# Order of steps, block places and branch-weight slots in the mixer part of a two-block transformer kernel

## The chip, the cores and the metric

The kernel runs as one program on one core of a Trainium2 chip. The metric is device time in microseconds (us) of one execution, as the median of several. The engines' names are those of the profile: PE (matmul), PEld (its weight loads), DVE (VectorE), ACT (ScalarE), SP (the queue that issues nearly all DMAs).

## The reference, cut to what matters

The input is 256 tokens of 1024 float32. A first block of two layers is followed by a second block (latent attention, mLSTM, 16 experts). Only the first block's layers are touched:

```python
for layer in range(2):
    h = rms_norm(x, norm1_g[layer])
    cols = lambda lo, w: h @ w_in[layer][:, lo:lo + w]
    y_sb   = stick_breaking_attention(...)          # from cols(0, 768)
    y_rwkv = rwkv7_time_mix(cols(768, 1024), ...)   # recurrence over 256 tokens
    y_moba = moba_attention(...)                    # from cols(1792, 768)
    y_hgrn = hgrn2_mixer(...)                       # from cols(2560, 1024)
    merged = 0
    for n, y_n in enumerate((y_sb, y_rwkv, y_moba, y_hgrn)):
        gate = sigmoid(cols(3584 + n * 1024, 1024))
        merged += gate * (y_n @ w_branch[layer, n])     # w_branch: 256 x 1024
    x = x + merged @ w_out[layer]
    h2 = rms_norm(x, norm2_g[layer])
    x = x + (silu(h2 @ w_ffn_gate) * (h2 @ w_ffn_up)) @ w_ffn_down
```

RWKV's recurrence is computed in two chunks of 128 tokens. Each needs the inverse of a unit lower triangular 128x128 matrix per head; it is built by doubling: from D (the diagonal blocks of 2) to blocks of 128 in six levels. HGRN's pair scores are built over eight levels of block size.

## The kernel before

All matrices lie with features on the 128 partitions and tokens along the row. `w_in` is multiplied in three products of a high and a low part (`group3`): ACT copies a weight block to the rounded high part (`block_high`), DVE subtracts to get the low part (`block_low`), PE multiplies. A *block* is 128 columns of `w_in`, all 1024 rows (1024 floats a partition). Two blocks come in one DMA of 1 MB to a *quarter slot*. There are four of these: the halves of ring slots 0 and 1. Slot 2 holds high parts only, in four block places up to block 28 (`TWO_PLACES`); from there on in two places, and its other half (slot `HALF`) takes first the weights of branch 1 and then, one after the other, the rows of `w_mod_2` that the second block will need (`modulation`; 8 loads in layer 0, 16 in layer 1). Low parts replace the weights in the quarter slot.

A layer runs so:

1. RWKV's 8 input blocks (unsplit float32, line 1223), with RWKV's first steps at places given by `EARLY_STEPS`, and on ACT and DVE the splits of the first blocks.
2. `mix([rw], fill, RW_PLAN)`: RWKV's steps, one at a time. After each, as many *fill steps* as the plan says. A fill step is half a unit of the other input columns: 12 matmuls of 256 columns on PE; on ACT and DVE what goes with it (an eviction, the high part of a block ahead, the low part of a block ahead). Steps 0 to 9 are first steps, keys, masks; 24 steps are the doubling; 8 the end of RWKV.
3. `branch(l, 1)`: RWKV's result by its branch weights.
4. `mix([hgrn, stick, moba], fill, MX_PLAN[l])`: the three other mixers in turn, one step of each, with fill steps between, now also modulation steps (`woven`: one after every 4 fill steps in layer 0, after every 2 in layer 1).
5. `branch` 0, 2, 3, then `w_out`, then the feed-forward jobs.

Every engine has its own program, written in the same order of steps by the same `mix` and plans; nothing is reordered at run time. An engine waits where its next instruction needs another's result, and all that is written behind it waits too. `take` gives PSUM banks in turn and waits for the bank's last reader. In `sync_program`, `load` takes the least recently used slot of the allowed ones and waits until what it holds has been used; SP issues strictly in the order written. Before branches 0, 2 and 3 are loaded, `ring_of` returns to the three full slots. So branch 0 goes to slot 0 (`held[0] = held[QUARTERS[1]]`: the last gate weights of that quarter), the next to slots 1 and 2, and `w_out` waits for the branches that use those slots.

In the row names, `ring` is loaded weights, `rring` the split high and low parts, `rgates` and `rarena` the split input, `ps` a PSUM bank, `high` and `low` the working memory.

## Time and profile before

| | us |
|---|---|
| median of 3 runs | 2205.24 (2203.21 to 2205.80) |
| profiled execution | 2205.08 |
| its span | 2203.3 |
| PE busy | 1869.2 (85%) |
| DVE busy | 908.7 (41%) |
| ACT busy | 639.8 (29%) |

Layer 0 runs from 0 to about 651 us of the span, layer 1 to about 1300 us; the second block follows, and its experts are the last third, in which 16 DMA engines are busy most of the time. In the two layers PE is busy in nearly every slice, and no single other engine is. A busy PE counts pipelined matmuls up to their modelled ends, so the idle time ahead of an instruction, with what ended it, tells more than the share.

### The profile page before, as it was taken

Reading aid. Unit: us, or ns where it says so; the run is one execution under the profiler, and the core shown is the slowest. Engines: PE = TensorE matmul, PEld = TensorE weight load, DVE = VectorE, ACT = ScalarE, POOL = GpSimd, SP = SyncE. Lnnn points to the kernel's source line nnn. Section 1 sums busy time; section 2 is a strip of 40 time slices with the busy share of each in tenths; the row PEclk is TensorE's granted clock in tenths of the full one; section 3 lists DMA queues with packets and bytes.
Section 4 is the critical chain, followed back from the end, with each engine's and each line's share of the span. In section 5 each row is a group of like instructions: output and inputs, shape, how many; then the busy total and the mean of one; then the engine's idle time right before and its main releaser. Section 6 shows DMA issues by size and latency. Waiting matters only on the chain.

```text
span 2203.3 us, 28203 instructions
## 1 busy us (share of the span) xinstructions
PE 1869.2 (85%) x12094; PEld 1447.0 (66%) x12094; DVE 908.7 (41%) x1432; ACT 639.8 (29%) x900; POOL 0.2 (0%) x4
## 2 busy tenths in 40 slices
PE   6899888899998899788999999998999875555555
PEld 5799776699996898666799999545788521111101
DVE  3665453556635754443546665413344300000001
ACT  3423242144433322322144454333442210000000
POOL 0000000000000000000000000000000000000000
PEclk9999999999998999997999999999999998887888
DMA  6323340555433323651565451121026899999997
GB/s 214 128 97 112 118 153 20 180 186 188 164 125 103 108 96 115 209 174 70 207 191 165 171 158 63 60 74 39 6 74 235 354 409 409 409 409 409 409 409 302
DMA packets 199645, 414.27 MB, mean 188 GB/s; under 512 B 5472, under 2 KB 119392, under 8 KB 196064
## 3 DMA queue, kind: packets, MB, share of 16 engines
q1 hardware_dynamic: 198800, 408.69, 51.0%
q10 hardware_dynamic: 720, 3.78, 0.4%
q8 instruction: 95, 1.56, 0.3%
q14 instruction: 30, 0.25, 0.0%
HBM read 411.41 MB, written 1.05 MB: 187 GB/s over the span
## 4 chain that ended last, share of the span: by engine, by line
PE 51%; DMA 21%; DVE 16%; ACT 9%; issue 2%; SPq 1%; DVEq 0%; ACTq 0%
PE ps L219 37%; PE ps L825 7%; DVE rarena L178 5%; ACT rarena L213 5%; DMA ring<-in_w_e_down_dram 5%; DMA high<-in_w_e_up_dram 4%; DMA high<-in_w_e_down_dram 3%; DVE low L178 3%; DVE high L178 3%; PE ps L1585 2%; DMA high<-in_w_e_gate_dram 2%; DMA ring<-in_w_e_gate_dram 2%; ACT high L213 2%; DMA ring<-in_w_mod_dram 2%; DVE high L188 1%
## 5 line engine op out<-in xcount | busy, mean ns | idle before, releaser
L219 PE MATMUL ps<-rarena 128*128 128x256 f32 (+1 forms) x3648 | 459.9, 288 | 9.6 <-DVE rarena L178 7.4
L219 PEld LDWEIGHTS ps<-rarena 128*128 128x128 f32 x3648 | 448.2, 192 | 19.6 <-DVE rarena L178 10.4
L219 PE MATMUL ps<-rgates,rring 128*128 128x256 f32 x1472 | 313.7, 301 | 5.3 <-DVE rring L178 5.3
L213 ACT ACTIVATE high<-ps 128x512 f32<-128x512 f32 (+2 forms) x226 | 109.3, 484 | 623.0 <-PE ps L1585 286.7
L219 PEld LDWEIGHTS ps<-rgates,rring 128*128 128x128 f32 x1472 | 250.1, 200 | 21.2 <-issue 14.0
L1585 PE MATMUL ps<-high,low 128*32 128x512 f32 x1040 | 162.4, 755 | 111.6 <-DMA high<-in_w_e_up_dram 38.3
L178 DVE TENSOR_TENSOR rarena<-ring,rarena 128x2048 fp32r<-128x2048 f32 x76 | 167.3, 2201 | 137.5 <-ACT rarena L213 135.9
L219 PE MATMUL ps<-rarena,rring 128*128 128x256 f32 x736 | 214.9, 292 | 0.0
L213 ACT ACTIVATE rarena<-ring 128x2048 fp32r<-128x2048 f32 x76 | 139.9, 1841 | 150.0 <-DMA ring<-in_w_ffn_up_dram 85.7
L1585 PEld LDWEIGHTS ps<-high,low 128*32 128x32 f32 x1040 | 31.4, 126 | 227.8 <-issue 59.7
L825 PE MATMUL ps<-high 128*128 128x128 f32 (+6 forms) x1024 | 131.5, 304 | 36.8 <-DVE high L178 32.2
L178 DVE TENSOR_TENSOR high<-high,ps 128x512 f32<-128x512 f32 x52 | 35.7, 687 | 301.0 <-PE ps L1585 266.6
L219 PEld LDWEIGHTS ps<-rarena,rring 128*128 128x128 f32 x736 | 147.7, 201 | 0.5 <-issue 0.5
L825 PEld LDWEIGHTS ps<-high 128*128 128x128 f32 (+2 forms) x1024 | 110.6, 196 | 50.5 <-DVE high L178 21.1
L219 PE MATMUL ps<-low,ring 128*128 128x256 f32 (+1 forms) x544 | 128.6, 393 | 16.3 <-DMA ring<-in_w_branch_dram 9.8
L178 DVE TENSOR_TENSOR rring<-ring,rring 128x1024 fp32r<-128x1024 f32 x104 | 127.4, 1225 | 32.5 <-ACT rring L213 23.5
L219 PE MATMUL ps<-high,ring 128*128 128x256 f32 (+1 forms) x544 | 132.8, 396 | 0.9 <-ACT low L213 0.9
L213 ACT ACTIVATE rring<-ring 128x1024 fp32r<-128x1024 f32 x104 | 110.1, 1059 | 80.2 <-PE ps L219 74.9
L1585 PE MATMUL ps<-ring,low 128*32 128x512 f32 x496 | 78.8, 768 | 58.8 <-DMA ring<-in_w_e_down_dram 20.1
L219 PEld LDWEIGHTS ps<-low,ring 128*128 128x128 f32 (+1 forms) x544 | 99.7, 190 | 43.8 <-DMA ring<-in_w_branch_dram 10.2
L219 PE MATMUL ps<-high 128*128 128x64 f32 (+7 forms) x576 | 123.5, 353 | 4.7 <-DVE high L192 3.9
L219 PEld LDWEIGHTS ps<-high,ring 128*128 128x128 f32 x544 | 100.8, 190 | 28.1 <-issue 11.4
(159 smaller groups left out, 1705.4 us busy)
## 6 DMA issues: line engine op xcount, KB each, us to landing
ring<-in_w_in_dram SPq DMA_DIRECT2D x66, 1024.0 KB, 5.2
high<-in_w_e_gate_dram SPq DMA_DIRECT2D x22, 2048.0 KB, 23.9
high<-in_w_e_up_dram SPq DMA_DIRECT2D x22, 2048.0 KB, 23.9
high<-in_w_e_down_dram SPq DMA_DIRECT2D x21, 2048.0 KB, 24.1
ring<-in_w_mod_dram SPq DMA_DIRECT2D x24, 1024.0 KB, 4.9
ring<-in_w_ffn_gate_dram SPq DMA_DIRECT2D x22, 1024.0 KB, 5.4
ring<-in_w_ffn_up_dram SPq DMA_DIRECT2D x22, 1024.0 KB, 8.0
ring<-in_w_e_down_dram SPq DMA_DIRECT2D x11, 2048.0 KB, 24.2
```

Of the source, the lines that this page charges most:

```text
L178: return self.e.tensor_tensor(out, x, y, op)
L188: return self.e.scalar_tensor_tensor(out=out, in0=x, scalar=s, in1=y, op0=op0, op1=op1)
L213: return self.e.activation(out, x, f, scale=scale, **kw)
L219: ins = self.e.matmul(out, l, r, start=first and i == 0, stop=end and i == n - 1)
L825: return PE.e.matmul(out, l, r, start=True, stop=True)
L1585: ins = PE.e.matmul(bs[ch][32 * e_:32 * e_ + 32, :], lhs(k, e_), w[:, e_, 512 * ch:512 * ch + 512], start=k == 0, stop=k == 7)
```

## The change

`EARLY_STEPS` and `RW_PLAN` steps of RWKV come ahead of the splits in the input loop on ACT and DVE, and the splits there start one turn (ACT) or two turns (DVE) later. DVE's keys move from two steps before the copies to a place right behind the bonus product. D is made in two halves, each with a name of its own (`D00`, `D01`). `TWO_PLACES` goes from 28 to 32. Branch 1 and then branches 0, 2 and 3 are loaded to quarter slots in turn; the full slots follow for `w_out` and the feed-forward weights. `RW_PLAN` gives 18 fill steps in the doubling where it gave 24; `MX_PLAN` gives fewer in the first rounds of the mixers and three to each step from the 28th on. HGRN has an empty step before its last product on each engine.

```diff
-        assert len(BLOCK) == BLOCKS and first_block["g00"] == TWO_PLACES
+        assert len(BLOCK) == BLOCKS and first_block["g01"] == TWO_PLACES
...
@@ sync_program
-            def branch(l, n, at=None):
+            def branch(l, n):
                 load(f"{l}b{n}", (lambda t: t[:, 0:2048].rearrange("p (k n) -> p k n", k=2),
-                                  a["w_branch"][l, n].rearrange("(k p) n -> p k n", p=128)), at=at)
+                                  a["w_branch"][l, n].rearrange("(k p) n -> p k n", p=128)))
...
                 for n, ch in GATES[0:3]:
                     gate(l, n, ch)
+                branch(l, 1)
                 held[HALF] = f"{l}blk{TWO_PLACES - 1}.used"
-                branch(l, 1, at=HALF)
                 mods = modulation(l)
...
-                ring_of[0] = range(NSLOT)
-                held[0], held[1] = held[QUARTERS[1]], held[QUARTERS[3]]
-                held[2] = f"{l}fill.used"
                 for n in (0, 2, 3):
                     branch(l, n)
+                ring_of[0] = range(NSLOT)
+                held[0], held[1], held[2] = held[QUARTERS[1]], held[QUARTERS[3]], f"{l}fill.used"
+                for i in (2, 1 - l, l):
+                    recent.remove(i)
+                    recent.append(i)
@@ hgrn of tensor_program and of scalar_program; in vector_program behind placed(7)
                     yield
+                yield
@@ scalar_program, input loop
-                    if 4 <= n < 7:
-                        block_high(l, n - 4)
                     if n in EARLY_STEPS[l]:
                         next(rw)
+                    if n > 4:
+                        block_high(l, n - 5)
@@ vector_program, rwkv
                 V.tt(R.bo, v2(ps(f"{l}bo.ps")), R.v, mul).then_inc(*V(f"{l}bo"))
                 yield
-                yield
                 V.wait_ge(f"{l}ee")
...
                 V.tt(R.KB[:, 1, :, :], R.k, R.en, mul).then_inc(*V(f"{l}KB"))
+                yield
                 yield
...
-                V.tt(R.D, R.Lm, bc8(c("lev", 0)), mul).then_inc(*V())
-                V.tt(R.D, R.D, bc8(c("ident")), add).then_inc(*V())
-                V.tt(R.DT, R.M4[:, :, 0:128], bc8(c("levt", 0)), mul).then_inc(*V())
-                V.tt(R.DT, R.DT, bc8(c("ident")), add).then_inc(*V(f"{l}D00", f"{l}D01"))
+                bc4 = lambda z: z.unsqueeze(1).to_broadcast([128, 4, 128])
+                for z in range(2):
+                    h = slice(4 * z, 4 * z + 4)
+                    V.tt(R.D[:, h, :], R.Lm[:, h, :], bc4(c("lev", 0)), mul).then_inc(*V())
+                    V.tt(R.D[:, h, :], R.D[:, h, :], bc4(c("ident")), add).then_inc(*V(f"{l}D0{z}"))
+                for z in range(2):
+                    h = slice(4 * z, 4 * z + 4)
+                    V.tt(R.DT[:, h, :], R.M4[:, h, 0:128], bc4(c("levt", 0)), mul).then_inc(*V())
+                    V.tt(R.DT[:, h, :], R.DT[:, h, :], bc4(c("ident")), add).then_inc(*V(f"{l}DT0{z}"))
@@ vector_program, input loop
-                    if n in (4, 5):
-                        block_low(l, n - 4)
                     if n in EARLY_STEPS[l]:
                         next(rw)
+                    if n > 5:
+                        block_low(l, n - 6)
@@ tables
-BLOCKS, TWO_PLACES = 52, 28
+BLOCKS, TWO_PLACES = 52, 32
-RW_PLAN = [3, 4, 3, 4, 3, 1, 1, 1, 1, 3] + 24 * [1] + [1, 1, 1, 1, 1, 2, 2, 3]
-MX_PLAN = 13 * [2] + [1], 22 * [2] + [1]
+RW_PLAN = [3, 4, 3, 4, 3, 1, 1, 1, 1, 3] + 6 * [1, 1, 0, 1] + [1, 1, 1, 1, 1, 2, 2, 3]
+MX_PLAN = [2] + 26 * [1] + [3], 9 * [2, 1, 1] + [3]
```

DVE's order in layer 0 around the keys (the reciprocal of 128x4 and the seven instructions behind it are the keys; `rring<-ring,rring` is a low part; the first row is the bonus product; the last two are the gated columns and the start of the forget gates):

```order
 L178 TENSOR_TENSOR high<-ps,high 128x512
-L178 TENSOR_TENSOR rring<-ring,rring 128x8x128 x2
+L178 TENSOR_TENSOR rring<-ring,rring 128x8x128
+L196 RECIPROCAL high<-high 128x4
+L188 SCALAR_TENSOR_TENSOR high<-high 128x2x128
+L178 TENSOR_TENSOR high<-high 128x2x128
+L188 SCALAR_TENSOR_TENSOR high<-high 128x2x128
+L178 TENSOR_TENSOR high<-high 128x2x128
+L178 TENSOR_TENSOR high<-high 128x512 x3
+L178 TENSOR_TENSOR rring<-ring,rring 128x8x128
 L188 SCALAR_TENSOR_TENSOR high<-high,ps 128x256 x2
 L200 MEMSET low 128x2
```

Before, the keys stood 15 rows behind the bonus product, after the forget gates' preparation and one more low part; now they are two rows behind it, and one of the two low parts follows them.

DVE's order in the doubling of layer 0, two levels. Before (`high<-ps,low` evicts an X with its mask, `high<-high,ps` adds to D or DT):

```order
L178 TENSOR_TENSOR high<-ps,low 128x512
L178 TENSOR_TENSOR high<-high,ps 128x512 x2
L178 TENSOR_TENSOR rring<-ring,rring 128x8x128
L178 TENSOR_TENSOR high<-high,ps 128x512 x2
L178 TENSOR_TENSOR high<-ps,low 128x512
L178 TENSOR_TENSOR rring<-ring,rring 128x8x128
L178 TENSOR_TENSOR high<-ps,low 128x512
```

The same place after:

```order
L178 TENSOR_TENSOR high<-ps,low 128x512
L178 TENSOR_TENSOR high<-high,ps 128x512 x4
L178 TENSOR_TENSOR rring<-ring,rring 128x8x128
L178 TENSOR_TENSOR high<-ps,low 128x512 x2
L178 TENSOR_TENSOR rring<-ring,rring 128x8x128
L178 TENSOR_TENSOR high<-high,ps 128x512 x4
```

The low part between the additions has gone, and three low parts stand where two levels had four.

DVE's order in layer 0 at HGRN's end (`high<-ps 128x256 x2` takes the last level, `high<-ps 128x512` HGRN's product, `low<-ps 64x256` a head of stick or MoBA, `low<-ps 2x512` the modulation's rows):

```order
-L192 COPY low<-ps 2x512 x4
+L178 TENSOR_TENSOR rring<-ring,rring 128x8x128
 L192 COPY high<-ps 128x256 x2
+L178 TENSOR_TENSOR rring<-ring,rring 128x8x128
+L192 COPY low<-ps 64x256
+L178 TENSOR_TENSOR rring<-ring,rring 128x8x128
+L192 COPY low<-ps 64x256
+L178 TENSOR_TENSOR rring<-ring,rring 128x8x128
 L192 COPY high<-ps 128x512
 L178 TENSOR_TENSOR high<-high 128x512
```

Three low parts and two heads now lie between HGRN's last level and its product, and the copies of the modulation's rows come later. SP's queue has the same DMAs in the same order before and after; only what each waits for differs.

## Rows read from the trace of the kernel before

**Rows 1.** The page: its head and section 1.

```profile
span 2203.3 us, 28203 instructions
PE 1869.2 (85%) x12094; PEld 1447.0 (66%) x12094; DVE 908.7 (41%) x1432; ACT 639.8 (29%) x900; POOL 0.2 (0%) x4
```

**Rows 2.** Timeline of PE: start, duration, engine, instruction, [idle before <- releaser].

```profile
43.60 0.76 PE L825 MATMUL ps<-low,high 65*128 65x256 f32 x1 [8.62 <-DVE high L200]
```

**Rows 3.** Timeline of DVE, layer 0, before that wait's end.

```profile
41.85 1.23 DVE L178 TENSOR_TENSOR rring<-ring,rring 128x1024 fp32r<-128x1024 f32 x1
43.19 0.27 DVE L200 MEMSET high<- 1x256 f32 x1
```

**Rows 4.** Timeline of PE, layer 0: the copies of keys, the first X.

```profile
99.79 0.47 PE L821 MATMUL ps<-cst,high 128*128 128x128 f32 x1 [6.91 <-DVE high L178]
...
126.69 0.38 PE L825 MATMUL ps<-high 128*128 128x128 f32 x1 [2.73 <-DVE high L178]
```

**Rows 5.** Timeline of DVE, layer 0: keys, mask products, D.

```profile
89.09 0.42 DVE L188 SCALAR_TENSOR_TENSOR high<-high,ps 128x256 f32<-128x256 f32 x1 [3.05 <-ACT high L213]
...
97.13 0.43 DVE L178 TENSOR_TENSOR high<-high 128x256 f32<-128x256 f32 x1
...
108.19 0.69 DVE L178 TENSOR_TENSOR high<-ps,cst 128x512 f32<-128x512 f32 x1 [1.57 <-PE ps L825]
...
110.88 0.69 DVE L178 TENSOR_TENSOR high<-ps,cst 128x512 f32<-128x512 f32 x1 [1.20 <-PE ps L825]
...
121.63 1.23 DVE L178 TENSOR_TENSOR high<-high,low 128x1024 f32<-128x1024 f32 x1
```

**Rows 6.** Windows, PE instructions with tile rring (fill steps), in the doubling.

```profile
127.00:192.00 65.00, 40.08 (x288) 1.00 0.27 89
```

**Rows 7.** Timeline of PE, layer 0, last fill steps before branch 1.

```profile
224.63 0.55 PE L219 MATMUL ps<-rgates,rring 128*128 128x256 f32 x1 [2.66 <-DVE rring L178]
```

**Rows 8.** Windows: PE, PEld, DVE, ACT, POOL busy (instructions), granted clock, DMA.

```profile
229.00:310.00 81.00, 72.09 (x533) 60.80 (x534) 39.30 (x66) 30.43 (x46) 0.00 (x0) 0.96 0.45 156
310.00:395.50 85.50, 67.40 (x457) 55.73 (x455) 33.12 (x57) 21.21 (x38) 0.00 (x0) 0.92 0.15 53
867.00:950.00 83.00, 70.19 (x523) 55.64 (x522) 38.88 (x69) 27.10 (x42) 0.00 (x0) 0.98 0.52 178
950.00:1043.00 93.00, 77.97 (x537) 61.26 (x535) 36.95 (x62) 24.52 (x43) 0.00 (x0) 0.89 0.34 116
994.00:1007.50 13.50, 13.50 (x61) 9.99 (x60) 1.89 (x6) 2.41 (x4) 0.00 (x0) 0.55 0.13 39
```

**Rows 9.** Timeline of PE: waits in the mixers.

```profile
297.49 0.38 PE L825 MATMUL ps<-high 64*128 64x128 f32 x2 [0.53 <-DVE high L178]
...
343.46 0.38 PE L825 MATMUL ps<-high 64*128 64x128 f32 x2 [3.56 <-DVE high L178]
...
357.04 0.32 PE L219 MATMUL ps<-high 128*128 128x64 f32 x1 [3.89 <-DVE high L192]
...
379.14 0.33 PE L821 MATMUL ps<-cst,high 128*128 128x128 f32 x1 [1.94 <-DVE high L183]
...
993.12 0.59 PE L825 MATMUL ps<-high 64*128 64x128 f32 x2 [3.52 <-DVE high L178]
...
1025.67 0.33 PE L821 MATMUL ps<-cst,high 128*128 128x128 f32 x1 [2.28 <-DVE high L183]
```

**Rows 10.** Timelines of SP's queue and of PE: loads of branch weights.

```profile
390.57 0.89 SPq L690 DMA_DIRECT2D ring<-in_w_branch_dram  x2
...
395.53 0.80 PE L219 MATMUL ps<-low,ring 128*128 128x256 f32 x1 [5.00 <-DMA ring<-in_w_branch_dram]
...
1043.05 0.79 PE L219 MATMUL ps<-low,ring 128*128 128x256 f32 x1 [4.84 <-DMA ring<-in_w_branch_dram]
```

**Rows 11.** Waits: engine, who waited for whom, us in total, times, longest.

```profile
PE ps L878 <- DMA ring<-in_w_mod_dram: 6.7, 7, 1.8
```

**Rows 12.** Timeline of ACT, behind the exponentials, a high part.

```profile
89.15 1.06 ACT L213 ACTIVATE rring<-ring 128x1024 fp32r<-128x1024 f32 x1
```

More of the change, by code:

```diff
@@ L2235, in rwkv @@
                 V.tt(R.KB[:, 1, :, :], R.k, R.en, mul).then_inc(*V(f"{l}KB"))
+                yield
                 yield
@@ L2378, in hgrn @@
                 placed(7)
+                yield
                 V.wait_ge(f"{l}hy.ps")
```

## The prediction

> **What bounds the kernel now.** I read the page first: PE is busy 85% of the span, DVE 41% [rows 1]. The last third is the expert stage, where weights stream in; nothing in it is edited, so it only starts earlier or later. I then listed every PE wait above 0.25 us in the PE timeline from 0 to 1280 us. The feed-forward jobs wait about 0.5 us apiece and are untouched. What is left is the mixer part of each layer, and I cut it by windows. The doubling (127 to 187 us) has no PE idle at all; between branch 1 and branch 0 PE idles 8.9 and 18.1 us in layer 0, 12.8 and 15.0 us in layer 1, which is each window less its PE busy time [rows 8]. Since PE's work does not change, the whole question is how much PE idle time goes or comes. I take layer 0 for the working and say where layer 1 differs.
>
> **1. First steps ahead of the splits.** PE waits 8.62 us for the one-row memset of RWKV's first step [rows 2]; on DVE a low split of 1.23 us stands right before it [rows 3]. Moved behind it, the memset comes 1.3 us earlier, in both layers. But DVE then has three low splits in a row where two stood, ahead of the operand of PE's next RWKV product, the norm of the keys; block 1's split, which DVE did early while it waited, is the third. 1.3 us won, 1.23 us more in front of the operand: I take 0. Bounds: 0 to -1.3 us a layer.
>
> **2. Keys ahead.** PE waits 6.91 us for the keys in layer 0 [rows 4], less in layer 1. The keys' eight instructions take 4.2 us on DVE; their last four are the 2.61 us that end at 99.74, 0.05 before PE goes on. Their operand, the exponentials of ACT, is there at about 89.1, since ACT is at its next instruction by 89.15 [rows 12] and DVE takes up work at 89.09 [rows 5]. So they end at 93.3 us and PE's wait shrinks to some 0.5 us. That is not the gain. In this stretch DVE is the later engine: from 89.09 on it waits for nothing but 1.21 us for ACT, and the split that came before and now comes behind the keys fills those. The other moved work only changes places, and PE next waits for the two splits behind the keys (an estimate of 0.3 and 2.3 us in layer 0). What PE's lead is worth is DVE's own waits for PE that follow, at the mask products: 1.57 and 1.20 us [rows 5]. They go: -2.8 us. Bounds: nothing, to the full 6.91.
>
> **3. D in halves.** Four instructions of 1.23 us become eight of 0.69 [rows 5]: with the 0.03 us between instructions 5.04 becomes 5.76, +0.7 us on DVE. PE's 2.73 us wait in front of the first X [rows 4] goes, but PE then only waits two steps later for X's own evictions, which stand behind all eight instructions and one split; I count no gain. Parts 2 and 3 together: -2.1 us a layer, -4.2 in all. The Trainium skill, "VectorE: DVE Perf Modes", section on the errata, says that each VectorE instruction reading SBUF pays a fixed latency that a large tile pays once and many small ones each; it speaks against this edit, and the trace agrees: half the elements take 56% of the time, not half. By its rule the edit costs 4 x 0.15 us a layer, the 0.7 of rows less the spacing; nothing in the sum hangs on it.
>
> **4. Doubling with 18 fill steps for 24.** A fill step is 12 matmuls, 40.08 us / 24 = 1.67 us, some 1.5 where it overlaps its neighbours [rows 6]. Six of them leave: the doubling gets 9 us shorter and the mixers 9 us longer, net 0. Is PE still covered? Without the fill step between the two D/DT groups a level has 11.0 - 1.5 = 9.5 us of PE work; DVE has six adds or products of 0.69 and on average one and a half splits of 1.23 in it, about 6.5 us, and each X is evicted while PE works through a fill step. I take no new wait; the bound is 0.5 us a level, +6 for both layers.
>
> **5. Four block places until block 32.** Before, PE waits 2.66 us in layer 0, and as long in layer 1, for a split that DVE has behind RWKV's last evictions [rows 7]: blocks 28 to 31 already run on two places, one ahead. With four places to block 31 and only 58 instead of 64 fill steps before branch 1, that split is long done. -5.3 us. Branch 1's weights, in a quarter slot now, need units 24 and 25 used; six fill steps and RWKV's last products, over 12 us, still lie between that and branch 1, and such a load takes about 5 us from issue to use (390.57 to 395.53 [rows 10]).
>
> **6. Branch weights.** The three loads of branches 0, 2 and 3 are issued together at 390.57, when the last fill unit has been used, and PE waits 5.00 us in layer 0 and 4.84 in layer 1 [rows 10]. In quarter slots the load of branch 0 only needs units 44 and 45 used and comes in SP's queue behind the last modulation load; in both layers four mixer steps or more of three fill steps remain, over 15 us. Both waits go: -9.8 us. The two halves of w_out are issued later than these and PE does not wait for them before either.
>
> **7. Fill moved from the first chains to the last.** Layer 0 gives two steps, then one to each of 26 mixer steps, then three; layer 1 gives two to each HGRN step and one to the others, for 9 rounds, then three. At the end PE waits 3.89 (HGRN's last product), 1.94 and, in layer 1, 2.28 us (transposes of MoBA) [rows 9]; three fill steps, 4.5 us, cover each, and HGRN's product has a step of its own in between: -8.1 us. Against it stand HGRN's middle levels. A level's product waits for a chain that begins with the MoBA step before it and goes over DVE and ACT; with one fill step there instead of two it can lose at most one fill step of cover, 1.67 us [rows 6], and nothing where the removed fill step takes its own splits (1.06 us ACT [rows 12], 1.23 us DVE [rows 3]) out of that same chain. Four levels in layer 0 and eight in layer 1 lose one: 0 to +20 us. I take half a fill step, 0.8 each: +9.6. That the price is between is seen in the first chains of before, which with two fill steps still wait 0.53 us where layer 0's later ones with one wait 3.56 [rows 9]. For the last steps, where only two block places are left and the chain of high part and low part (1.06 + 1.23 and what stands between in two queues) is nearly as long as a unit of two fill steps, 3.0 us, I add +2.
>
> **8. Modulation loads.** They share one half slot; in layer 1 PE waits for them 7 times, 6.7 us [rows 11]. With 4 fill steps a round instead of 6 the next load has time in the first nine rounds; in the last seven, at three fill steps a step, I leave 2.5 us. -4.2.
>
> **9. The clock.** After long waits PE is granted its lower level (1.2 of 2.4 GHz): behind the 3.52 us wait at 993.12 [rows 9] the granted clock is 0.55 for 13.5 us [rows 8], which is 12 us at the low level and 6 lost. The means of 0.92 and 0.89 in the two late windows are 14 and 21 us at it. The long waits at the end go, shorter ones come: -2 us. The Trainium skill, "TensorE: Matmul & The Clock Gate", section on HAM oscillation, states that a wait re-throttles the array each time and that the penalty is half the throttled time; the trace agrees on both here.
>
> Sum: -4.2 - 5.3 - 9.8 - 8.1 + 9.6 + 2 - 4.2 - 2 = -22.0 us. The profiled execution took 2205.08 us (span 2203.3 and 1.8 around it), the median of the runs is 2205.24, so both lead to 2183.
>
> **The rivals.**
> A, *cover lost in full*: every one of the twelve levels loses a whole fill step (20 instead of 9.6), the doubling waits 0.5 us a level (+6), part 2 brings nothing (+5.6 back). -22 + 22 = 2205, no change. For it: DVE and ACT order splits and chains rigidly. Against: splits leave with the fill steps.
> B, *the chains get shorter*: levels lose no cover because their own splits are gone (-9.6), and the clock stays up in layer 1's end (-5): 2168. For it: at 297.49 a wait of half a microsecond is all there is.
> C, *the clock turns it slower*: PE in the mixers has fewer fill steps between waits, and the low level spreads from the late windows to the whole of both mixer parts, some 330 us. They now have 44 us at the low level (twice what each window's clock lacks to 1, times its length [rows 8]), a mean clock of 0.94. At 0.83 it would be 112, 68 us more, half of it lost: +34, 2217. It decides from about 0.87 down, where the 22 us are used up. For it: 0.89 in the window with one to two fill steps a step; against: 0.92 in layer 0's late window, with one a step throughout, which is what the plan gives everywhere.
> D, *a load is late*: branch 1's weights or branch 0's are stuck behind a waiting load in SP's queue and 5 us stay per layer: 2193.
> E, *it does not do what it says*: the waits for branch and splits remain through a release I misread; within 4 us of before.
>
> **How the numbers follow.** Forecast 0.58 (own range 2174 to 2191), A 0.09, B 0.13, C 0.05, D 0.11, E 0.04. B and the forecast's upper side give 2166 as the low end; D, and half of A, give 2197 as the high end, with 2 in 10 outside. The runs of this kernel differ by 0.12%, so 0.2%, 4.4 us, is what can be told. Faster: forecast, B, D and half of A with the mildest part of C, 0.87; within 0.2%: the rest of A and E, 0.08; slower 0.05.
>
> **What would show it.** Right: no PE wait for w_branch before branch 0, no wait for a split right before branch 1, PE's wait before the key copies under 1 us with DVE's waits at the mask products gone, branch 1 some 13 us earlier in layer 0, no wait at HGRN's last product. Wrong: PE waits in the doubling; HGRN level waits above 2 us more than before on average; rring waits in the last rounds; a granted clock below 0.9 in both mixer parts.

## The result, and the profile after

| | us |
|---|---|
| median of 5 runs | 2192.85 (2191.08 to 2194.93) |
| kernel before, same chip, 5 runs | 2203.21 (2198.38 to 2205.80) |
| ratio | 0.9955, 95% interval 0.9939 to 0.9971 |
| span of the profiled execution | 2191.1 (before 2203.3) |

The change makes the kernel 10 us faster, where 22 were forecast. A second set of 12 runs of it (run 12 below) gave 2197.91 and a ratio of 0.9971 (0.9959 to 0.9984), 5.6 us less than the kernel before beside it. The direction holds; the size is less than half of the forecast.

PE has the same number of instructions as before and is as busy [rows 1], in a span 12.2 us shorter (the last row, of the page's section 6, is the loads of modulation rows: count, size, median us from issue to landing):

```profile
span 2191.1 us, 28206 instructions
...
PE 1867.4 (85%) x12094; PEld 1444.1 (66%) x12094; DVE 909.7 (42%) x1440; ACT 639.9 (29%) x900; POOL 0.2 (0%) x4
...
ring<-in_w_mod_dram SPq DMA_DIRECT2D x24, 1024.0 KB, 4.9
```

PE's timeline after (start, duration, instruction, idle before it and its releaser), with the places of [rows 2, 4, 7, 9, 10] in the same order:

```profile
42.36 2.04 PE L827 MATMUL ps<-low,high 65*128 65x256 f32 x4 [6.87 <-DVE high L200]
...
95.87 0.38 PE L219 MATMUL ps<-rgates,rring 128*128 128x256 f32 x1 [1.12 <-DVE high L188]
...
100.85 0.36 PE L219 MATMUL ps<-rgates,rring 128*128 128x256 f32 x1 [1.87 <-DVE rring L178]
...
121.50 1.16 PE L827 MATMUL ps<-high 128*128 128x128 f32 x8 [0.59 <-DVE high L178]
...
130.11 5.37 PE L827 MATMUL ps<-high 128*128 128x128 f32 x32 [3.71 <-DVE high L178]
...
213.39 0.66 PE L823 MATMUL ps<-cst,high 128*128 128x128 f32 x4 [3.35 <-DVE high L178]
...
366.32 0.91 PE L823 MATMUL ps<-cst,high 128*128 128x128 f32 x3 [3.88 <-DVE high L183]
...
387.45 7.24 PE L219 MATMUL ps<-low,ring 128*128 128x256 f32 x30 [0.57 <-issue]
...
1032.17 7.37 PE L219 MATMUL ps<-low,ring 128*128 128x256 f32 x31
```

The wait for the one-row memset is 6.87 us for 8.62. The 6.91 us in front of the key copies are gone; 1.12 and 1.87 stand right behind them. The first X comes 5.2 us earlier than in [rows 4], yet the first D/DT products behind it now wait 3.71 us, and their 32 matmuls take 5.37 us where later levels take 3.73: PE is at its lower clock. DVE's waits at the mask products (1.57 and 1.20 us, [rows 5]) are gone, as forecast. Branch 1 starts 10.9 us earlier in layer 0 (218.16 for 229.06; 7.6 in run 12), where some 13 were expected. Before RWKV's last transposes PE waits 3.35 us; the split wait of 2.66 us [rows 7] is gone. At the transposes of MoBA the 1.94 us of [rows 9] have become 3.88. Branch 0 waits for no DMA in either layer (5.00 and 4.84 in [rows 10]), and its products got faster too: the 40 matmuls behind the old waits took 11.07 and 11.44 us and take 9.64 and 9.56 now; the lower clock that came with those waits is gone there. Before:

```profile
395.53 11.07 PE L219 MATMUL ps<-low,ring 128*128 128x256 f32 x40 [5.00 <-DMA ring<-in_w_branch_dram]
...
1043.05 11.44 PE L219 MATMUL ps<-low,ring 128*128 128x256 f32 x40 [4.84 <-DMA ring<-in_w_branch_dram]
```

The mixer parts of layers 0 and 1 (windows as in [rows 8], here the whole part: length, PE busy, then PEld, DVE, ACT; granted clock, DMA share, GB/s), and the wait for modulation rows that answers to [rows 11] (total, times, longest):

```profile
218.20:387.50 169.30, 147.32 (x1058) 124.09 (x1057) 74.83 (x124) 53.88 (x88) 0.00 (x0) 0.94 0.37 128
843.70:1032.20 188.50, 159.97 (x1127) 128.01 (x1126) 78.29 (x132) 53.45 (x87) 0.00 (x0) 0.93 0.46 160
```

```profile
PE ps L880 <- DMA ring<-in_w_mod_dram: 14.2, 8, 4.5
```

Before, they took 166.4 us (139.4 busy) and 175.6 (147.8 busy). Both now carry six more fill steps, 9 us by the forecast's count. Layer 0's is 2.9 us longer, near what the forecast's terms give (9 - 5.0 - 5.8 + 3.2 + 1 = +2.4); layer 1's is 12.9 longer, for +5 (9 - 4.8 - 2.3 + 6.4 + 1 - 4.2, before the clock). From the layer's start to branch 0, layer 0 gained 8.1 us, layer 1 only 1.3; the products of branch 0 brought 1.4 and 1.9 more. The wait for modulation rows was to fall from 6.7 to 2.5 and rose to 14.2. What it is made of is seen in SP's queue and on PE, around the longest and at a late one:

```profile
968.67 0.33 SPq L690 DMA_DIRECT2D ring<-in_w_mod_dram  x1
969.04 3.83 SPq L690 DMA_DIRECT2D ring<-in_w_in_dram  x2
974.60 0.34 SPq L690 DMA_DIRECT2D ring<-in_w_mod_dram  x1
```

```profile
982.90 1.57 PE L880 MATMUL ps<-ring,low 128*2 128x512 f32 x8 [4.52 <-DMA ring<-in_w_mod_dram]
...
1011.13 1.04 PE L880 MATMUL ps<-ring,low 128*2 128x512 f32 x8 [1.20 <-DMA ring<-in_w_mod_dram]
```

The half slot is used until 974.5 (a modulation step from 973.50, 1.04 us long). The next load is issued at 974.60, behind two gate loads of 1 MB of which the first went out at 969.04, and its matmuls start at 982.90: 8.3 us. Later there are no gate loads left, but 1006.15 us (the issue) to 1011.13 is still 5.0 us, and between two modulation steps PE has one mixer step (0.4 to 1 us) and two fill steps (3.1 us). Of the 14.2 us, 2.8 are the first row block (883.86, issued behind gate loads), 0.7 the rest of the first rounds, and 10.6 the last seven modulation steps (1.88, 1.04, 4.52, none, 0.35, 1.20 and 1.65 us).

### The profile page after: what moved, and what is told of

It is laid out like the page before. It is cut to its first block, busy times and chain, and to the rows that moved or that the text cites. A ratio compares the mean times of both kernels' runs of the same rounds, so it can differ in the third digit from the quotient of the medians.

```text
span 2191.1 us, 28206 instructions
## 1 busy us (share of the span) xinstructions
PE 1867.4 (85%) x12094; PEld 1444.1 (66%) x12094; DVE 909.7 (42%) x1440; ACT 639.9 (29%) x900; POOL 0.2 (0%) x4
## 4 chain that ended last, share of the span: by engine, by line
PE 51%; DMA 21%; DVE 17%; ACT 8%; issue 2%; SPq 1%; DVEq 0%; ACTq 0%
PE ps L219 37%; PE ps L827 7%; DMA ring<-in_w_e_down_dram 5%; DMA high<-in_w_e_up_dram 4%; DVE rarena L178 4%; ACT rarena L213 4%; DVE high L178 3%; DVE low L178 2%; PE ps L1588 2%; DMA ring<-in_w_e_up_dram 2%; DMA ring<-in_w_mod_dram 2%; DMA high<-in_w_e_down_dram 2%; DMA high<-in_w_e_gate_dram 2%; DMA ring<-in_w_e_gate_dram 2%; DVE rring L178 2%
## 5 line engine op out<-in xcount | busy, mean ns | idle before, releaser
L219 PE MATMUL ps<-rgates,rring 128*128 128x256 f32 x1472 | 306.6, 298 | 4.4 <-DVE high L188 2.3
L213 ACT ACTIVATE high<-ps 128x256 f32<-128x256 f32 (+2 forms) x226 | 109.3, 484 | 645.9 <-PE ps L1588 286.6
L219 PEld LDWEIGHTS ps<-rgates,rring 128*128 128x128 f32 x1472 | 244.8, 197 | 20.5 <-issue 9.6
L1588 PE MATMUL ps<-high,low 128*32 128x512 f32 x1040 | 162.4, 757 | 111.4 <-DMA high<-in_w_e_up_dram 40.0
```

Source lines behind the costliest of these rows:

```text
L213: return self.e.activation(out, x, f, scale=scale, **kw)
L219: ins = self.e.matmul(out, l, r, start=first and i == 0, stop=end and i == n - 1)
L1588: ins = PE.e.matmul(bs[ch][32 * e_:32 * e_ + 32, :], lhs(k, e_), w[:, e_, 512 * ch:512 * ch + 512], start=k == 0, stop=k == 7)
```

## The experiments

Times are medians, and a ratio is the time over that of the kernel before, run beside it; that one had 2203.5 to 2206.5, so that times of different runs carry some 3 us of difference between their sets. Theories and rivals are those of the text put on record ahead of each run. "Part" is a part of the forecast, "after" the changed kernel. An edit of 1 to 3 us is read in the trace, not in the time; run 12 shows why. A layer's length runs from the start of the span (layer 0) or from its first RWKV input product (layer 1) to branch 0.

**Run 1, branch weights alone** (the kernel before, with the change's `branch` and its place in the queue):

```diff
-                branch(l, 1, at=HALF)
+                branch(l, 1)          # a quarter slot; 0, 2, 3 likewise, before ring_of returns to the full slots
```

> The kernel before, with only the branch weights taken to quarter slots (part 6 of the forecast). Forecast: both waits of PE in front of branch 0 (5.00 and 4.84 us) go and nothing else changes, about 2195, 9.8 us less. Rival 1: in layer 1 the wait only moves, because gate loads and modulation loads in SP's queue now stand behind branch 1's quarter (a quarter is taken out of the turn): waits for modulation rows grow, 2198 to 2203. Rival 2: the loads are on the path through the queue to w_out, which is then waited for: no change. Seen by the PE waits for w_branch, for w_mod and for w_out.

2198.74 us, ratio 0.997 (0.9956 to 0.9984). No wait for w_branch or w_out is left, as forecast. The mixer parts, layers 0 and 1:

```profile
228.70:390.00 161.30, 139.28 (x987) 116.50 (x986) 72.44 (x122) 51.26 (x83) 0.00 (x0) 0.94 0.35 124
860.10:1040.50 180.40, 155.26 (x1055) 123.32 (x1054) 75.83 (x130) 51.23 (x83) 0.00 (x0) 0.89 0.45 158
```

Layer 0's gains 5.1 us over before. Layer 1's is 4.8 longer although PE idles less in it (25.1 us for 27.9): modulation rows 8.6 us (6.7 before; the new 1.8 is the first row block, behind a gate load that now needs branch 1's quarter), and the same instructions keep PE busy 155.3 us for 147.8, at a clock of 0.89 for 0.93. Rival 1 had the wait and the time right; the larger part of the lost gain is the clock, in this one execution (the 12 runs lie between 2189.5 and 2204.9 us).

**Run 2, no modulation loads in layer 1** (after; not computed: 15 of the 16 row blocks of the modulation in layer 1):

```diff
                     for k in range(8):
+                        if l and (g3, k) != (1, 0):   # take the first block's slot and landing, load nothing
+                            table[f"mod{g3}{k}"], slot_of[f"mod{g3}{k}"] = table["mod10"], HALF
+                            yield
+                            continue
```

> The kernel after, with the 15 modulation loads of layer 1 behind the first left out: the modulation steps multiply the rows that already lie there, so that part of the modulation is not computed; the instructions of every compute engine stay as they are. Theory 1 (the single half slot costs layer 1 its gain): the waits for w_mod, 14.2 us in layer 1, fall to at most 3 (the first load), and most of it is kept, since those waits stand in the last rounds where nothing else is late: mixer part of layer 1 188.4 to 177 to 180 us, time about 2183. Theory 2 (the chains with less cover cost it, and a wait for a load only stands where a wait for a chain would): waits for DVE in those rounds grow by nearly as much, mixer part above 185 us, time 2190 or more. Theory 3 (the clock): as theory 2, with the low level in other stretches.

2177.84 us, ratio 0.9872 (0.9853 to 0.9892), 15 us below after's first set and 20 below its second. Layer 1's mixer part, and its wait for modulation rows:

```profile
844.80:1016.90 172.10, 155.45 (x1125) 124.55 (x1125) 78.30 (x132) 53.49 (x87) 0.00 (x0) 0.94 0.24 82
```

```profile
PE ps L884 <- DMA ring<-in_w_mod_dram: 2.8, 1, 2.8
```

16.4 us shorter: 11.4 us of waits, and 4.5 of PE time for the same instructions, at a clock of 0.94 for 0.93. The waits for DVE and ACT did not grow (12.2 and 1.6 us, for 12.8 and 1.6 in after). Theory 1 holds, 2 and 3 fall; the part came out below the 177 to 180 us expected, by the clock.

**Run 3, even plans** (part 7 undone in after):

```diff
-MX_PLAN = [2] + 26 * [1] + [3], 9 * [2, 1, 1] + [3]
+MX_PLAN = 19 * [2] + [1], 28 * [2] + [1]
```

> The kernel after, with even plans for the mixers: layer 0 two fill or modulation steps to each of 19 mixer steps, then one; layer 1 two to each of 28, then one. This undoes part 7 alone (the number of steps stays 55 and 64). Forecast of the prediction: the last products and transposes are waited for again (8.1 us), the middle levels get their cover back in layer 1 (half of 9.6): slower than after by 0 to 4 us. Theory 1 of the modulation loads: with two steps to a mixer step a modulation step comes every one and a half mixer steps, as before, so the waits for w_mod in layer 1 fall from 14.2 to about 7, as in the kernel before; layer 1 gains 3 to 6 us, layer 0 loses up to 4. Theory 2 of the chains: the waits at HGRN's levels fall by 5 us or more in layer 1.

2181.20 us, ratio 0.9893 (0.9877 to 0.9910): 11.7 us faster than after (16.7 than run 12), where the forecast had 0 to 4 slower. The profiled execution, the slowest of the five, is 7.6 us shorter than after's; in it layer 0 gains 1.3 us, layer 1 5.3. Its waits for modulation rows:

```profile
PE ps L880 <- DMA ring<-in_w_mod_dram: 11.4, 8, 2.9
```

So the plan of the change, alone, costs more than it brings. Of the sizes, 11.4 us is between the 7 of theory 1 and the 14.2 of after: even spacing helps, but does not make the loads fit. Layer 1's mixer part is 7.2 us shorter, 2.8 of it by these waits, 3.3 by PE time for the same instructions (156.6 us for 159.9, clock 0.94 for 0.93), the rest by other waits. Theory 2 falls: layer 1's waits for DVE stay at 12.5 us (12.8 in after).

**Run 4, D whole** (after, part 3 undone):

```diff
-                for z in range(2): ...      # two instructions each for D and DT, on half z
+                V.tt(R.D, R.Lm, bc8(c("lev", 0)), mul).then_inc(*V())
+                V.tt(R.D, R.D, bc8(c("ident")), add).then_inc(*V())
+                V.tt(R.DT, R.M4[:, :, 0:128], bc8(c("levt", 0)), mul).then_inc(*V())
+                V.tt(R.DT, R.DT, bc8(c("ident")), add).then_inc(*V(f"{l}D00", f"{l}D01", ...))
```

> The kernel after, with D and its transpose built again by four instructions of 128x1024 in place of eight of 128x512 (part 3 undone). Forecast of the prediction: the halves cost DVE 0.7 us a layer and PE gets nothing for it, so D whole is 0.7 us a layer faster: the wait of 3.71 us at the first D/DT products shrinks by 0.7 although the first X is waited for some 2 us longer. Rival: the halves let PE do the first X early, which frees DVE's evictions earlier; D whole then makes the D/DT products later by 0.5 to 1.5 us a layer. Either way below 0.2% of the time: to be read in the start of the D/DT products (130.11 and 756.35 in the kernel after).

2204.08 us, ratio 0.9993 (0.9969 to 1.0018). DVE here: the last instruction for D, and the evictions of the two X; then PE: the first X and the first D/DT products.

```profile
124.39 1.22 DVE L178 TENSOR_TENSOR high<-high,cst 128x1024 f32<-128x1024 f32 x1
...
127.78 0.69 DVE L178 TENSOR_TENSOR high<-ps,low 128x512 f32<-128x512 f32 x1 [0.83 <-PE ps L827]
...
131.81 0.69 DVE L178 TENSOR_TENSOR high<-ps,low 128x512 f32<-128x512 f32 x1 [2.01 <-PE ps L827]
```

```profile
125.67 2.07 PE L827 MATMUL ps<-high 128*128 128x128 f32 x8 [4.17 <-DVE high L178]
...
133.05 3.73 PE L827 MATMUL ps<-high 128*128 128x128 f32 x32
```

With halves the D/DT products start at 130.11, 130.60 and 130.78 us (after, run 12, run 11), here at 133.05; in layer 1, counted from its start, at 114.1 there and 116.6 here. Until then the halves gain about 2.5 us a layer, where the forecast had a loss of 0.7. DVE does lose 0.7, but here PE only begins X when all of D is there, and DVE then waits 0.83 and 2.01 us for PE before it can evict; with halves it waits for neither. Most of it is lost again at once: with halves these products stand behind a wait of 3.71 us and run at the lower clock. The next X starts at 136.75, 137.33 and 137.51 us with halves (after, run 12, run 11) and at 138.06 here,

```profile
138.06 1.05 PE L827 MATMUL ps<-high 128*128 128x128 f32 x8
```

and 120.6 to 121.6 us into layer 1, here 121.6: 0.6 to 1.3 us are left in layer 0, 0 to 0.9 in layer 1. The time can't tell (12 runs from 2193.6 to 2226.1 us; the highest had a mean clock of 0.89).

**Run 5, keys late** (after, part 2 undone):

```diff
                 yield
+                yield
                 V.wait_ge(f"{l}ee")
...
                 V.tt(R.KB[:, 1, :, :], R.k, R.en, mul).then_inc(*V(f"{l}KB"))
-                yield
                 yield
```

> The kernel after, with DVE's keys at their old place, two steps before they are needed (part 2 undone). Forecast of the prediction: PE waits for the keys again (6 to 7 us in layer 0 where it waits 1.12 and 1.87 us now), and the part as a whole loses 2.8 us a layer until the first D/DT products (start of layer to those products: 130.1 and 114.1 us in the kernel after). Rival: between the exponentials and the first D/DT products DVE has no idle time now, so the 4.15 us that it waits for ACT before the keys are all that can be lost: with the keys late DVE does the gated columns and splits in that time, and the loss is below 1 us.

2201.47 us, ratio 0.9981 (0.9967 to 0.9996). PE waits 6.9 and 3.8 us for the keys again. The D/DT products start at 132.58, and 115.8 us into layer 1: 1.8 to 2.5 us and 1.7 us later. The forecast (2.8) is nearer than the rival (below 1).

**Run 6, both plans of before** (after, parts 4 and 7 undone):

```diff
-RW_PLAN = [...] + 6 * [1, 1, 0, 1] + [...]
-MX_PLAN = [2] + 26 * [1] + [3], 9 * [2, 1, 1] + [3]
+RW_PLAN = [...] + 24 * [1] + [...]
+MX_PLAN = 13 * [2] + [1], 22 * [2] + [1]
```

> The kernel after, with both plans of before (24 fill steps in the doubling; 13 rounds and 22 steps of two in the mixers): parts 4 and 7 undone, the rest kept. Forecast of the prediction: doubling 9 us longer and mixers 9 us shorter a layer, HGRN's last product waits its 3.9 us again, the levels get cover back: slower than after by 8.1 less 9.6 less 2 = within 4 us of it. Theory of the modulation loads (from the runs so far: 14.2 us of waits in layer 1, worth 16 us of its mixer part): with two steps to a mixer step early and one late, waits for w_mod fall to about 8.6 as in the kernel before with quarter slots, mixer part of layer 1 188.4 less 9 less 6 us, and the time 2184 to 2189, faster than after.

2183.50 us, ratio 0.9890 (0.9871 to 0.9908), as run 3. Layers 385.3 and 383.4 us, in run 3 386.2 and 384.6: moving six fill steps a layer out of the doubling is worth about nothing either way, as part 4 said. The waits for modulation rows are 9.0 us in layer 1, as the theory had them (8.6). HGRN's last product does not wait here either (a split in front of it does, 1.0 us), although the plan is that of before: so it is not the plan that covers the 3.89 us, and the empty step is what is left. MoBA's transposes at the end, 1.94 and 2.28 us in [rows 9], wait little in both layers too:

```profile
374.93 0.55 PE L823 MATMUL ps<-cst,high 128*128 128x128 f32 x3 [0.56 <-DVE high L183]
...
1014.08 0.55 PE L823 MATMUL ps<-cst,high 128*128 128x128 f32 x3 [0.56 <-DVE high L183]
```

So nearly the whole gain that part 7 expected at the ends of the chains is there without the new `MX_PLAN`. Whether the empty step or the block places bring the transposes early was not separated.

**Run 7, two places for modulation rows** (after; in layer 1 one quarter leaves the gates' turn):

```diff
+                    spare = next(i for i in recent if i in QUARTERS)
+                    ring_of[0] = [i for i in QUARTERS if i != spare]
...                  # loads in the order in which their places come free
+                            load(f"mod{g3}{k}", ..., at=spare if c > 1 and c % 2 == 0 else HALF)
```

> The kernel after, with a second place for modulation rows in layer 1: one of the four quarter slots is taken out of the gates' turn while they run, and modulation loads go to it and to the half slot in turn; gate weights run on three quarters. All loads are done, nothing is left out. Theory 1 (one place, loaded only after its last use, makes PE wait): waits for w_mod fall from 14.2 to about 3 us (the first), the mixer part of layer 1 from 188.4 to 172 to 176 us, time 2177 to 2181. Rival: the waits come from the bytes (a modulation row block behind two gate loads takes 8 us to land in place of 5), so that more buffers help little or the gates are late now: waits for w_mod or w_in above 8 us, time 2186 or more.

2181.52 us, ratio 0.9889 (0.9872 to 0.9905). Layer 1's mixer part and its wait for modulation rows:

```profile
841.30:1012.70 171.40, 154.19 (x1126) 123.78 (x1125) 78.29 (x132) 53.47 (x87) 0.00 (x0) 0.95 0.50 176
```

```profile
PE ps L902 <- DMA ring<-in_w_mod_dram: 2.7, 1, 2.7
```

The bytes are the same, at 176 GB/s in place of 160, and the waits but the first are gone; three quarters are enough for the gates. The length (171.4 us) is that of run 2: it was the single place, not the bytes. The Trainium skill, "Trainium Kernel Development and Optimization", section Best Practices, tells to double-buffer so that DMA overlaps compute; this trace agrees, and [rows 11] add that the single place did less harm (6.7 us) while the steps stood wide apart.

**Run 8, three things together** (run 7, run 3, and two more fill steps in the doubling's first level):

```diff
-RW_PLAN = [3, 4, 3, 4, 3, 1, 1, 1, 1, 3] + 6 * [1, 1, 0, 1] + [...]
+RW_PLAN = [3, 4, 3, 4, 3, 1, 1, 1, 1, 3] + [1, 3, 0, 1] + 5 * [1, 1, 0, 1] + [...]
```

> The kernel after with three things that the runs point to: two places for modulation rows in layer 1; even plans for the mixers (two fill or modulation steps to each mixer step until 19 and 28); and two more fill steps in the doubling's first level ([1, 3, 0, 1]), where PE waits 3.71 us before the first D/DT products. Expected: that wait falls to about 0.5 us in both layers (the two fill steps are taken from the mixers: 3 us off each layer's sum, and less low clock behind it), waits for w_mod about 1 us, mixer part of layer 1 about 165 us (181.2 of the even plan less 11.4 of waits, less 3.3 of fill). In all 2181 - 10 - 6 = 2165. Rival: chain waits take the place of the modulation waits in the even plan: 2173. Rival: the three fill steps in one place bring three splits of DVE with them in front of its evictions, and the D/DT products are as late as before: 2171.

2174.14 us, ratio 0.9858 (0.9842 to 0.9875). The first D/DT products of layer 0:

```profile
130.49 3.73 PE L849 MATMUL ps<-high 128*128 128x128 f32 x32
```

Two fill steps more stand before them, they start as early as with after's plan (130.11 to 130.84 us), and run at the full clock (3.73 for 5.37 us). But the forecast of 2165 was missed, and its first rival (2173) came true: layer 1's mixer part is 177.4 us, with two fill steps fewer than run 7's 171.4. It waits 22.3 us for DVE and ACT, at HGRN's levels and MoBA, where run 7 waits 14.5; with the 2.3 us for modulation rows that is as much as run 3 waited in all (24.5). How much of this is the even plan and how much the two fill steps taken, run 9 tells.

**Run 9, the best of each** (run 8 with after's own plan in layer 1):

> Two places for modulation rows in layer 1 and two more fill steps in the doubling's first level, as in the run with all three; the even plan only in layer 0, and in layer 1 the changed kernel's own plan (9 rounds of 2, 1, 1, then three to each step). The traces say that the plan of the change is good in layer 1 once the modulation rows are there: 171.4 us for the mixer part with 60 fill steps (two places, its own plan) against 177.4 with two fill steps fewer (two places, even plan). Expected: mixer part of layer 1 about 168, the rest as in that run (2174.1): 2165 to 2169. Rival: the 177.4 comes from other places of the chains by chance of the two missing fill steps, and then 2172 to 2175.

2169.62 us (2169.34 to 2170.27), ratio 0.9843 (0.9829 to 0.9856): 35 us faster than before, 23 to 28 than after (2165 to 2169 expected). The mixer parts:

```profile
218.10:376.40 158.30, 141.45 (x1035) 118.20 (x1033) 73.69 (x123) 52.46 (x86) 0.00 (x0) 0.96 0.38 133
832.20:1004.50 172.30, 150.66 (x1102) 121.15 (x1101) 77.07 (x131) 52.44 (x86) 0.00 (x0) 0.96 0.49 171
```

Layer 1's takes 172.3 us, five less than in run 8, but not the 168 expected. It has two fill steps fewer than run 7's (171.4) and waits 20.7 us for DVE and ACT where that waits 14.5: the fill steps taken were cover. So of run 8's 7.8 us more of such waits, 6.2 go with the two fill steps, in part as the rival had it, and 1.6 with the even plan. The rest of the five is 1.9 us of waits for modulation rows and 1.6 of PE time at a better clock (0.96 for 0.94). That after's plan is the better one in layer 1 is shown for the time (4.5 us), less clearly for the cause.

**Run 10, splits first** (after, part 1 undone; DVE shown, ACT alike):

```diff
+                    if n in (4, 5):
+                        block_low(l, n - 4)
                     if n in EARLY_STEPS[l]:
                         next(rw)
-                    if n > 5:
-                        block_low(l, n - 6)
```

> The kernel after, with the splits of the first blocks ahead of RWKV's first steps again on ACT and DVE (part 1 undone). Forecast of the prediction: part 1 is worth nothing (bounds 0 to -1.3 us a layer): first RWKV product later by 1.3 to 1.5 us (42.36 in the kernel after), the key-norm product earlier by about as much (67.78), key copies and D/DT products within 0.3 us. Rival: the splits are what DVE has too much of from there to D, and put early they fill its idle time before 42 us: D/DT products 1 us earlier or more (130.11), and the time 2 to 4 us shorter.

2197.95 us, ratio 0.9965 (0.9951 to 0.9978). The D/DT products start at 129.22 us, 0.9 to 1.6 earlier, in layer 0, and 1.5 later in layer 1 (115.6 into it). The sum is nothing, as forecast, out of two opposite halves that were not.

**Run 11, copies behind the scalings** (after, one number of the plan):

```diff
-MX_PLAN = [2] + 26 * [1] + [3], ...
+MX_PLAN = [2] + 26 * [1] + [2, 3], ...
```

> The kernel after, with two fill steps in place of three at the 28th mixer step of layer 0 (MX_PLAN[0] = [2] + 26 * [1] + [2, 3]). By it the last modulation step of layer 0, and with it DVE's four copies of the modulation row (2x512 each, 2.85 us together), comes behind MoBA's scalings of a head on DVE and not before them. Theory: the wait of 3.88 us at the transposes of MoBA (366.32 in the kernel after) comes from these copies, and falls below 1 us; mixer part of layer 0 169.3 to about 166. Rival: the scalings are late for another reason (ACT's splits), and a wait of 2 us or more stays there or one step later.

2191.07 us, ratio 0.9950 (0.9932 to 0.9969). DVE in after (the copies of the modulation row, then MoBA's reciprocal):

```profile
362.50 2.85 DVE L192 COPY low<-ps 2x512 f32<-2x512 f32 x4 [2.30 <-PE ps L880]
365.39 0.17 DVE L196 RECIPROCAL high<-high 128x2 f32<-128x2 f32 x1
```

and here, with layer 0's mixer part (window columns as above):

```profile
361.39 0.17 DVE L196 RECIPROCAL high<-high 128x2 f32<-128x2 f32 x1
...
363.91 2.85 DVE L192 COPY low<-ps 2x512 f32<-2x512 f32 x4 [1.64 <-PE ps L880]
```

```profile
217.40:380.90 163.50, 144.32 (x1059) 120.73 (x1058) 74.87 (x124) 53.52 (x87) 0.00 (x0) 0.97 0.39 133
```

The 3.88 us wait is gone, a split is waited for 1.5 us, and the part is 163.5 us for 169.3 and 171.1 (run 12). Only 2.8 and 1.2 us of that are idle time of PE; the larger part is PE time for the same instructions (144.3 us for 147.3 and 150.7), at a clock of 0.97. The theory holds for the wait; the time is at the lower end of what after had (2191.1 to 2203.1 us).

**Run 12, after once more**:

> The changed kernel once more, beside the kernel before in the same turn, to see how far its own time and its clock move from one set of runs to the next. If single edits of 1 to 3 us can be told by the time, it is at 2192.9 within 2 us. If the low clock moves by itself (the run with D whole had times from 2193.6 to 2204.7 of one kernel, at mean clocks of 0.943 to 0.937), it lies between 2190 and 2200 with a spread of 5 us or more.

2197.91 us (2191.24 to 2203.10, 12 runs), ratio 0.9971 (0.9959 to 0.9984). Its mixer parts:

```profile
221.50:392.60 171.10, 150.69 (x1059) 126.90 (x1057) 74.88 (x124) 53.89 (x88) 0.00 (x0) 0.92 0.36 124
849.60:1039.90 190.30, 162.36 (x1126) 129.77 (x1125) 78.30 (x132) 53.49 (x87) 0.00 (x0) 0.90 0.45 156
```

The same program waits about the same (20.4 and 27.9 us, 22.0 and 28.5 in after), but PE is busy 150.7 and 162.4 us where it was 147.3 and 160.0, at clocks of 0.92 and 0.90 for 0.94 and 0.93. So edits of 1 to 3 us can't be told by the time.

## Why the prediction was right in direction and wrong in size

| term | forecast | measured in the trace |
|---|---|---|
| 1 to 3, until the first D/DT products | -4.2 | -5.2 |
| 4, doubling | 0 | 0 (runs 3 and 6) |
| 5, wait before branch 1 | -5.3 | -3.3 |
| 6, branch weights | -9.8 | -9.3 |
| 7, waits at the end of the chains | -8.1 | -4.2 |
| 7, middle levels and last steps | +11.6 | +1.6 |
| 8, modulation rows | -4.2 | +7.5 |
| 9, clock | -2.0 | +0.7 (what is left) |
| sum | -22.0 | -12.2 (span) |

**The step that failed is part 8.** "With 4 fill steps a round instead of 6 the next load has time in the first nine rounds; in the last seven, at three fill steps a step, I leave 2.5 us." The three fill steps include a modulation step, so each mixer step of the last rounds carries one. The sum to be made was: 4.9 us for a load (page, section 6 of after) against one mixer step and two fill steps, 3.5 to 4.1 us: about 1 us short wherever the mixer step is a short one. Nor did it count the gate loads ahead in SP's queue (8.3 us at 982.90, and the 2.8 us of the first row block). The last seven steps cost 10.6 us for the 2.5 forecast, the first nine rounds 3.5 for none. Runs 2 and 7 show the price: taking the wait away, in two ways, gives 11 to 15 us against after's first set, 16 to 20 against its second.

None of the signs named for a wrong forecast came (splits cost 0.3 us, the mixers' clocks were 0.94 and 0.93, the levels were not 2 us worse): none of them watched the modulation loads.

**Part 7's cost was put at the wrong place.** The levels of HGRN and MoBA lost almost nothing with one fill step for two (waits 16.2 to 17.5 and 14.1 to 14.4 us): what rival B said of the levels. It hid most of part 8's error, so that the span fell 12 us and not 2. The gain at the ends was half: HGRN's product 3.89 gone (not by the plan, run 6), layer 1's 2.28 gone (0.56 without the plan, run 6), but 1.94 in layer 0 became 3.88, through four copies of 2.85 us that the new plan puts before MoBA's scalings (run 11). The forecast counted fill steps as cover only, not what a moved modulation step brings onto DVE.

**Part 5**: the split right before branch 1 is early now, but the same work stands before RWKV's transposes (1.58 to 3.35 us in layer 0, 1.84 in layer 1; 3.4 in run 12). **Part 6** is right where it was read; it left out that branch 0's own products get 1.4 and 1.9 us shorter, and run 1 adds the clock that layer 1 can lose. **Parts 1 to 3**: the sum is right up to the start of the D/DT products; part 3 had the wrong sign there (run 4), which part 1's and 2's smaller gains hid, and at the lower clock these products give back 1.6 us or more a layer. **Part 4** is right: no PE wait in the doubling behind its first level, and the 3.71 us there do not come from the plan (run 6 has them too).

**The clock** was taken to gain from fewer long waits; the new ones of 3.5 to 4.5 us took that back (the two mixer parts together had 44 us at the lower level before, 48 in after and 65 in run 12, counted as in the prediction). The prediction priced the lower level at half its time. Here it cost a quarter to a half: between after and run 12, 6.8 us more of it in layer 0's mixers came with 3.4 us more PE time, 10.2 us in layer 1's with 2.5; between before and run 1, 17.8 us with 7.4. The Trainium skill, "TensorE: Matmul & The Clock Gate", section on HAM oscillation, has the array re-throttled by every long wait. The runs here agree on the long ones: behind 3.71 us before the D/DT products the low level came in after's trace and in runs 11 and 12 (5.37 to 5.47 us for 3.73), and so it did with each of the six long waits (3.55 to 4.52 us) in the mixers of after, and of run 12. They add that it also comes behind shorter ones, and not each time: behind 1.93 and 1.78 us at 276.3 and 287.8 in run 12, but not behind 1.95 and 1.77 us at the same places of after (273.9 and 283.8). So nearly the same list of waits in layer 0's mixers gave 0.94 once and 0.92 once.

## What to carry to other kernels

A plan that moves filler also moves the filler's own loads and evictions: for each stretch, put the load's time from issue to landing against the work between two uses of its buffer, and look at which chain the filler's vector work now stands in. A single buffer that costs little at an even pace costs its shortfall at most uses once the pace goes up; here a second place was then worth 11 to 16 us. Splitting an instruction can pay where a long chain of another engine starts from its first half, even if the total gets longer; look behind the chain's next wait, though, where most of the 2.5 us was gone here. And before a plan is credited with a wait that went, undo the plan alone (run 6).

## What was not expected of the hardware

The granted clock moves by itself: one program, 12 runs on one chip, gave 2191.2 us at a mean clock of 0.946 and 2203.1 at 0.938. The mean clock does not order the runs between these two (2192.0 us at 0.941, 2200.8 at 0.940), so it explains the spread only in part. Run 9's five runs, with fewer waits, lie within 1 us, though their mean clocks differ too (0.932 to 0.950). What starts one low stretch and not another behind equal short waits stays open.
